# Another start offset for each activation buffer against the weight buffers

## The reference

```python
# layer 0: h += even_mixer(rms(h)); h += conv_ffn(rms(h))
proj = hn @ w_in                          # 2048 -> 512 + 4*1536: u, q, k, v, g
y = concat([s5(u), retention(q, k, v, g)]) @ w_out_even
# layer 1: h += mla_mixer(rms(h)); h += conv_ffn(rms(h))
c = hn @ w_down; q = rms(cq) @ w_uq; kv = rms(ckv) @ w_ukv
o = softmax(mask(q k^T)) @ v; y = o @ w_out_odd
# conv_ffn: a = hn @ w_up (2048 -> 2*5632); width-3 causal conv; silu(gate)*val @ w_down
# final rms norm
```

## Time and profile before

| | |
|---|---|
| Median of 3 runs | 2285.14 us (2283.3 to 2286.89) |
| The profiled execution, its own time | 2288.69 us |
| Its span, first to last instruction | 2286.9 us |
| TensorE matmul busy | 2173.6 us, 95% |
| TensorE weight load busy | 2131.3 us, 93% |
| VectorE, ScalarE, GpSimd busy | 65%, 44%, 34% |
| DMA, mean | 174 GB/s |
| Mean granted TensorE clock | 0.979 |

### The profile page before, as it was taken

The page is one execution under the profiler, slowest core; times in us unless marked ns, Lnnn a source line. Parts: engine busy times, 40 slices in busy tenths (PEclk is TensorE's granted clock), DMA queues, the critical chain, the costliest instruction groups (busy, mean ns, idle before and its releaser), DMA issues.

```text
span 2286.9 us, 47346 instructions
## 1 busy us (share of the span) xinstructions
PE 2173.6 (95%) x18398; PEld 2131.3 (93%) x18398; DVE 1478.1 (65%) x1744; ACT 1003.2 (44%) x1244; POOL 784.3 (34%) x889
## 2 busy tenths in 40 slices
PE   7588888999999999999999999999999999999997
PEld 7587777999999999999999988999999999999997
DVE  7377777577766655666666666667666655666666
ACT  4233333444544444444444445444444444444442
POOL 5689997013334300434411000023434101434311
PEclk9899999999999999999999999999999999999998
DMA  6332333455545456555456533355555556555463
GB/s 258 111 121 110 134 115 123 174 186 190 198 183 202 168 193 225 189 198 187 173 188 203 185 116 119 132 185 193 193 183 196 176 191 209 203 197 187 164 201 113
DMA packets 64459, 398.69 MB, mean 174 GB/s; under 512 B 7152, under 2 KB 9712, under 8 KB 28784
## 3 DMA queue, kind: packets, MB, share of 16 engines
q1 hardware_dynamic: 60048, 391.15, 48.2%
q10 hardware_dynamic: 4320, 6.27, 0.8%
HBM read 395.29 MB, written 2.10 MB: 174 GB/s over the span
## 4 chain that ended last, share of the span: by engine, by line
PE 80%; POOLq 9%; POOL 5%; issue 3%; DVE 2%; ACT 0%; DVEq 0%; ACTq 0%
PE PS L1394 24%; PE PS L1395 24%; PE PS L1398 24%; POOLq L1281 2%; POOLq L1285 2%; POOL g L1283 2%; POOL E L1286 2%; POOLq L1153 2%; POOLq L1160 1%; PE PS L1389 1%; POOL S L1298 1%; PE PS L1390 1%; PE PS L1391 1%; POOLq L1299 1%; PE PS L1735 1%
## 5 line engine op out<-in xcount | busy, mean ns | idle before, releaser
L696 DVE TENSOR_TENSOR lo<-raw,hi 128x1024 fp32r<-128x1024 f32 (+2 forms) x826 | 951.1, 1171 | 545.0 <-ACT hi L351 540.1
L351 ACT ACTIVATE hi<-raw 128x1024 fp32r<-128x1024 f32 (+2 forms) x826 | 786.0, 969 | 728.1 <-PE PS L1398 684.0
L1394 PE MATMUL PS<-XS,hi 128*128 128x256 f32 x3584 | 852.6, 280 | 14.6 <-ACT hi L351 14.6
L1395 PE MATMUL PS<-XS,hi 128*128 128x256 f32 x3584 | 846.3, 278 | 0.0
L1394 PEld LDWEIGHTS PS<-XS,hi 128*128 128x128 f32 x3584 | 680.8, 190 | 22.7 <-issue 15.6
L1395 PEld LDWEIGHTS PS<-XS,hi 128*128 128x128 f32 x3584 | 681.0, 190 | 0.3
L1398 PE MATMUL PS<-XS,lo 128*128 128x256 f32 x3584 | 481.2, 277 | 0.0
L1398 PEld LDWEIGHTS PS<-XS,lo 128*128 128x128 f32 x3584 | 441.9, 188 | 0.0
L1395 PE MATMUL PS<-YF,hi 128*128 128x256 f32 x1408 | 331.8, 276 | 0.0
L1394 PE MATMUL PS<-YF,hi 128*128 128x256 f32 x1408 | 331.8, 276 | 0.0
L1351 POOL TENSOR_TENSOR ctmp<-apad,cws 128x512 f32<-128x512 f32 x88 | 131.9, 1520 | 525.9 <-DVE apad L747 525.9
(11 more groups left out here) (236 smaller groups left out, 2497.2 us busy)
## 6 DMA issues: line engine op xcount, KB each, us to landing
raw<-in_ffn_up SPq DMA_DIRECT2D x176, 1024.0 KB, 4.8
raw<-in_ffn_dn SPq DMA_DIRECT2D x128, 704.0 KB, 4.1
raw<-in_w_in SPq DMA_DIRECT2D x52, 1024.0 KB, 4.8
raw<-in_w_oe SPq DMA_DIRECT2D x16, 1024.0 KB, 4.8
raw<-in_w_oo SPq DMA_DIRECT2D x16, 1024.0 KB, 4.8
raw<-in_mla_dn SPq DMA_DIRECT2D x9, 1024.0 KB, 4.8
raw<-in_w_ukv SPq DMA_DIRECT2D x8, 1024.0 KB, 4.8
raw<-in_w_uq SPq DMA_DIRECT2D x8, 768.0 KB, 4.4
```

The costliest lines, as they stand in the source:

```text
L351: act.activation(hi[:, p % SLOTS, 0:n], raw[:, u % SLOTS, off:off + n], ACT.Copy).then_inc(hi_ready, 1)
L696: V.tensor_tensor(lo[:, p % SLOTS, 0:n], raw[:, u % SLOTS, off:off + n], f(hi[:, p % SLOTS, 0:n]), ALU.subtract).then_inc(lo_ready, 1)
L1394: mm(PS[:, bank, 0:T], wh, x[:, 0:T], start=first, stop=False)
L1395: mm(PS[:, bank, 0:T], wh, x[:, T:2 * T], start=False, stop=False)
```

## The change

It changes the size of one unused buffer and adds five. No instruction is added, removed or moved; only addresses change.

```diff
-        gap = sb("gap", [P, 80])
+        gap = sb("gap", [P, 64])
...
         even = ExitStack()
+        gap_e = sb("gap_e", [P, 112], fp32, even)
         YE = sb("YE", [P, 12, 2 * T], f32r, even)
+        gap_5 = sb("gap_5", [P, 16], fp32, even)
         s5o = ExitStack()
...
         odd = ExitStack()
+        gap_o = sb("gap_o", [P, 88], fp32, odd)
         YO = sb("YO", [P, KD, 2 * T], f32r, odd)
+        gap_c = sb("gap_c", [P, 16], fp32, odd)
         CS = sb("CS", [P, 2 * KR, 2 * T], f32r, odd)
...
         ffn = ExitStack()
+        gap_f = sb("gap_f", [P, 8], fp32, ffn)
         YF = sb("YF", [P, GK, 2 * T], f32r, ffn)
```

## The result

The changed kernel takes 2375.41 us (median of 4 runs, 2372.52 to 2375.72) where the one before took 2286.01 in the same comparison: a ratio of 1.0389, 95% interval 1.0371 to 1.0407. It is slower by 89 us, well outside the range that was forecast. The profiled execution has a span of 2373.8 us, 86.9 us more than before.

What follows compares the result with a forecast made beforehand. The prediction took TensorE's back-to-back matmuls as the bound, 17,760 times their start-to-start distance. All address terms were taken as 0, so the forecast stayed at the median, 2285.14 us, with an 80% range of 2274 to 2325.

Steps and rivals of the forecast that it cites:

- What bounds the kernel: TensorE, 95% busy with matmuls: time is a number of matmuls times the distance from one start to the next.
- The count of matmuls: Whole kernel, TensorE: 17,760 matmuls of 256 columns, counted from the low-by-high rows and the forms with three products together.
- the two distances of before: TensorE windows in the trace: 113.3 and 117.8 ns from start to start, no value between them lasting.
- Is it the address?: TensorE's weight-activation pairs: all at 192 bytes yet at two distances, so a fixed address relation can't by itself be the cause.
- Two offsets, one pair of values: Value products at 320, other matmuls at 192, records of similar two lengths: taken as evidence against dependence on the offset.
- a symmetrical dependence: Caveat for TensorE's offsets: 192 and 320 lie equally far from 0, so such a dependence would not show.
- The term for `XS`: `XS` matmuls, offset from 192 to 256: taken as 0; upper bound +37 us for 8,174 in the two long stretches.
- `YF`, bounded at +19: 4,224 feed-forward `YF` matmuls, offset from 192 to 224: taken as 0, upper bound +19 us.
- the rival's 2341 us: Slower case with both `XS` and `YF` in the two long stretches at the long distance: 2341 us.
- The slower rival: Weight load and preceding matmul's streaming clash in SBUF, the offset deciding how often: 2322 us with `XS` alone; chance 0.26.
- The sign that the prediction gave for it: If matmul length changes exactly where `XS` gives way to `YF` in one gapless run, the offset matters.
- The other engines: GpSimd, VectorE, ScalarE alignment: taken as 0, GpSimd's early S5 chain bounded at +-3 us; slower by alignment 0.02.

Runs made afterwards that it cites:

- raw64: Against the kernel before, only `raw` moved, 64 bytes down, all else staying in place: 2284.87 us, ratio 0.9997.
- xs256: Against the kernel before, only the shared gap cut from 320 to 256 bytes, putting `XS` at 256 against the weights: 2346.82 us, ratio 1.0262.
- shift: Against the kernel before, 32 unused bytes ahead of `H`, so every buffer moves and all distances stay at 192: 2285.82 us, ratio 0.9998.
- all0: Against the kernel before, `gap` dropped and 320 unused bytes put behind `nwt`, all six activation buffers at distance 0: 2385.26 us, ratio 1.0430.

## Why the prediction was wrong

- **What bounds the kernel: right.** The time moved with the distance from start to start, at TensorE: 78.4 of the 86.9 us are counted from it. The count of matmuls, the windows and the two distances of before hold.
- **The step that failed is "Is it the address?"** It saw that one distance of 192 bytes went with 113.3 and with 117.8 ns, and concluded that the offset is no cause. The two values at 192 are real, and neither is set by the offset alone: `YO` ran at 113.2 ns in `raw64` and in `xs256`, its distance unchanged. But that a quantity takes two values at one setting says nothing about its values at others. At 192 there is a choice of 113.3 and 117.8; at 256 there is only 120.0.
- **"Two offsets, one pair of values" was the wrong comparison.** 192 and 320 are 192 and 64 modulo 256, and of the twelve settings tried these are the only two at which 113.3 ns was seen at all. That the trace of before held just these two was bad luck. The hole that the prediction named, a symmetrical dependence, is not the one that was there: the table is not symmetrical.
- **The term for `XS` was taken at 0 and bounded at +37 us; it measured about +55 in the same two stretches.** The prediction took it at 0 because the offset was held to be no cause, and its bound took the longer of the two known distances, 117.8 ns, as the worst that there is. A value not in the trace, 120.0, was worse. `YF`, bounded at +19, cost 21. With both, the rival's 2341 us would still have been 34 short.
- **The slower rival was right that the offset decides**, and it had 0.26. The sign that the prediction gave for it, a change of length just where the buffer changes within one run of matmuls, is what the changed kernel shows: the last eight `XS` matmuls take 803.03 - 802.07 = 0.96 us, 120.0 ns each, and the first six `YF` steps 803.74 - 803.03 = 0.71 us, 118.3 each. That weight load and streaming clash in SBUF is a reading: the runs show that the address of the one relative to the other counts, and not what happens in the memory.

```profile
802.07 1.12 PE L1403 MATMUL PS<-XS,lo 128*128 128x256 f32 x8
803.03 0.28 PE L1399 MATMUL PS<-YF,hi 128*128 128x256 f32 x1
803.74 0.28 PE L1399 MATMUL PS<-YF,hi 128*128 128x256 f32 x1
```

- **The other engines: right for the time.** The early chain was to keep its length within 3 us, and the output projection behind it starts 2.7 us later; `shift` and `raw64` change the time by nothing beyond their intervals of some 0.1%. That GpSimd's multiply would get shorter and VectorE's write of `lo` longer was not foreseen, nor that part of the slowdown is hidden in the S5 stage under TensorE's waits.
- **The two rules of the Trainium skill.** SBUF - State Buffer, "Who interferes with whom", says that TensorE's read ports are independent and that it waits for no one. The runs disagree with no offset mattering, which the prediction took from it: the distance of TensorE's two operands is worth up to 4.3% of this kernel, `all0` against before. By the Trainium skill's TensorE: Matmul & The Clock Gate, "Wait - 56ns, not 53.3ns?", 256 columns take an estimate of 109.2 ns; no distance tried came under 113.3 with these fp32r matmuls.
- **Still open:** what makes 256 bytes the period and 192 the one setting at which the short distance lasts, and what tips a run at 192 or 64 into one of its two values. `YO` at 192 was short in the traces of `raw64` and `xs256`, in which `raw` starts 64 bytes lower, and long in those of before and `shift`; one trace of each shows no cause. Distances between 32-byte steps were tried only near 192.

## What to carry to other kernels

Where TensorE is bound by back-to-back matmuls that each load a tile, read the time from start to start by buffer before believing that it is at its floor: here it went from 113.3 to 120.0 ns with nothing changed but where two buffers lie to each other. A trace in which all pairs share one setting can't tell that the setting doesn't matter; a kernel in which each buffer has another one, like this changed kernel, shows in one run that it does. And a bound taken from the worst row in the trace is no bound for a setting that the trace doesn't hold.

## What the runs showed of the hardware

With fp32r operands of 256 columns and a stationary tile for each, TensorE's start-to-start time depends on (moving address - stationary address) modulo 256 bytes: at a granted clock of 1.00 it is 113.3 or 117.8 ns at 192 and at 64, 120.0 at 0, 119.7 to 120.0 at 96, and 116.6 to 119.0 at the other eight settings tried. At 192 the short value held through stretches of 6,177 and 6,221 matmuls and the long one through 790; at 64 the long one held in all the feed-forward windows read. Moving all buffers by 32 bytes (`shift` 0.9998) or moving `raw`, which TensorE does not read (`raw64` 0.9997), changed nothing.
